# Index scores moved into a projection slot, the key norm's root and its sums moved in their queues

## The chip, the core and the metric

The kernel runs on one core of a Trainium2 chip. Its engines run side by side and meet only at semaphores: TensorE (PE) multiplies, ScalarE (ACT) and VectorE (DVE) work on elements, GpSimd (POOL) helps with elements, SyncE (SP) starts transfers. The metric is the device time of one execution, in microseconds (us); lower is better. All numbers are float32. Where a product has to be exact to float32, both operands are split into a rounded part (fp32r) and the rest, and three products are added.

## The reference

Two model blocks follow one another on 256 tokens of width 1024. The change lies in the last attention of the second block, the sparse one (DSA); what matters of it:

```python
proj = h @ w_in                       # 1024 x 2376: c_q 256, k 1024, v 1024, k_idx 64, w_idx 8
c_q = rms_norm(c_q, cq_g)
q = (c_q @ w_uq).reshape(B, S, 16, 64)
q_idx = apply_partial_rope((c_q @ w_uq_idx).reshape(B, S, 8, 64), cos, sin)
k_idx = apply_partial_rope(rms_norm(k_idx), cos, sin)
q = apply_partial_rope(rms_norm(q, q_g), cos, sin) * (d ** -0.5)
k = apply_partial_rope(rms_norm(k.reshape(B, S, 16, 64), k_g), cos, sin)
# for each block of 128 queries
dots  = einsum('bqhe,bke->bqhk', q_idx, k_idx)            # 8 index heads
score = einsum('bqh,bqhk->bqk', w_idx, relu(dots))        # + causal mask by chunks of 64
vals, idx = top_k(score, 64)
p = softmax(q . k[idx])                                   # 16 heads
o = p . v[idx];   return o @ w_out
```

Before it stand the differential attention and its MLP (`mlp0`), behind it the output projection `o3` and the last MLP (`mlp1`).

## The kernel before

The order of all work is written out by hand, one program for each engine; each runs its own list from top to bottom, and a wait holds up everything that stands behind it on that engine.

**Slots.** A weight matrix is read in slots of 1024 x 512 (1 MB) into `ringA`, which holds two. ScalarE rounds half a slot to fp32r (`round_slot`, writes `Ah`), VectorE or GpSimd makes the rest `Al = ringA - Ah` (`rest_slot`), and TensorE multiplies (`split_slot`, L786 to L834): for each half, 8 products `hTh, Ah` (both token tiles `t`, four parts `k`), 8 products `hTl, Ah`, 8 products `hTh, Al`. The last product of a tile counts up `job_rdy`; ScalarE then takes the 128 x 512 result out of PSUM (`sin_out`) and counts up `job_out`. `Ah` has two halves, so the rounding of a half waits until TensorE is done with the same half of the slot before (`a_free`).

**The DSA projection** has five slots, `sin` 0 to 4 (slot 4 has 328 columns). Behind slot 1 come the queries and index queries from the latent (L1474). Inside slot 2, between its halves, TensorE turns the index queries and keys (`index_aside`). The keys `s_k` are columns of slots 0, 1 and 2, the values `s_v` of 2, 3 and 4. GpSimd makes `Al` of slots 3 and 4.

**Index scores and top-k.** For each of 8 index heads TensorE multiplies two pieces into PSUM bank `i % 3` (L1485, L1486), ScalarE applies Relu (L2040), and VectorE adds it with its weight to `s_acc` (L2921, L2923). The three hand on in a ring: head `i` on TensorE waits for the Relu of head `i - 3` (`ixr`), the Relu for VectorE's addition of head `i - 2` (`ixs`). VectorE then finds the 64 largest of each row in 8 rounds of `max` and `match_replace` (L2937, L2940), and makes the mask `s_sel` (L2943, L2944).

**Key norm.** ScalarE squares the keys (L2044, counts up `osq`); VectorE sums the squares per head (`head_sums`, L2798) ahead of top-k round 3; ScalarE takes the root (`head_root("sk", 1)`, the call of `root` at L1523); VectorE scales and rotates the keys (`head_scale`, `rope2`, ahead of round 6; L2804, L2807, L2699 to L2704). TensorE turns the result (`turn_blocks`, L1261) and the attention over 16 heads begins (L1277). Ahead of that turn stands filler, `keep(7, ...)`: seven products nobody reads (L759).

**Queries.** TensorE turns them inside slot 3 (`query_aside`); ScalarE copies them out with `turned_queries` (eight instructions of L1686), then come `sin_out(3)` and the rounding of slot 4's second half, and behind these the key norm's root.

Of the kernel before, what the change touches and what calls it, by code (L numbers as in the profile page):

```python
# [28 lines left out]
P = 128  # L29
T = 256  # L30
# [15 lines left out]
IDX_H = 8  # L46
# [36 lines left out]
def program(nc, d, out_d):  # L83
# [4 lines left out]
    with ctx:  # L88
# [41 lines left out]
        def col(name, k):  # L130
            return cols[:, COL[name][0] + k:COL[name][0] + k + 1]
# [57 lines left out]
        job_rdy = sem("job_rdy")  # L189
# [122 lines left out]
        def in_job(w, c):  # L312
            at, name = (4, "din2") if w == "din" else (2, "sin2")
            return J[name][0] + 2 * (c - at) if c >= at else J[w][0] + 2 * c
# [408 lines left out]
        def _(pe):  # L723
# [32 lines left out]
            def keep(n, b):  # L756

                for _ in range(n):
                    mm(ps[:, b, 0:T], ident, con[:, 0:T], start=True, stop=True)  # L759
# [5 lines left out]
            def job_bank(j):  # L765
                if j >= 4:
                    pe.wait_ge(job_out, j - 3)
                return bank(j)
# [14 lines left out]
                        j += 1  # L783
                    off += n

            def split_slot(a, banks, name=None, done=None, between=None):  # L786

                n = A[a][0][2]  # L790
                for half in range(2):
                    ks = range(4 * half, 4 * half + 4)
                    pe.wait_ge(ah_rdy, 2 * SPLIT[a] + half + 1)

                    def product(t, left, right, start=False, stop=False, ready=None, ks=ks):
                        for k in ks:
                            if ready is not None and name and t == 0 and k % 2 == 0:
                                pe.wait_ge(ready, 4 * TI[name] + k // 2 + 1)
                            ins = mm(ps[:, banks[t], 0:n], left[:, k, t * P:(t + 1) * P],  # L799
                                     right[:, half, (k % 4) * n:(k % 4) * n + n],  # L800
                                     start=(start and k == 0), stop=(stop and k == KT - 1))
                        return ins

                    if done is m_rdy and half == 1:
                        pe.wait_ge(al_rdy, 2 * SPLIT[a] + half + 1)
                        for t in range(NT):
                            product(t, hTh, Ah)
                            product(t, hTl, Ah)
                            product(t, hTh, Al, stop=True).then_inc(m_rdy, 1)
                        continue  # L810
                    if name and half == 0:
                        for k in ks:
                            for t in range(NT):
                                product(t, hTh, Ah, start=True, ready=ha_rdy, ks=[k])
                        pe.wait_ge(al_rdy, 2 * SPLIT[a] + 1)
                        for t in range(NT):
                            product(t, hTh, Al)
                        for t in range(NT):
                            last = product(t, hTl, Ah, ready=hv_rdy)
                    else:  # L820
                        for t in range(NT):
                            product(t, hTh, Ah, start=True, ready=ha_rdy)
                        for t in range(NT):
                            product(t, hTl, Ah, ready=hv_rdy)
                        pe.wait_ge(al_rdy, 2 * SPLIT[a] + half + 1)
                        for t in range(NT):
                            last = product(t, hTh, Al, stop=True)
                            if half == 1 and done is not None:
                                last.then_inc(done, 1)
                    if half == 0 or done is None:  # L830
                        last.then_inc(a_used, 1)
                    if half == 0 and between is not None:
                        between()
# [7 lines left out]
                split_slot(a, (0, 2), name="o%d" % n)  # L841
                split_slot(a + 1, (1, 3), done=m_rdy)

            def split_jobs(a, j0, name=None, between=None):
                banks = (0, 1) if name else (job_bank(j0), job_bank(j0 + 1))
                split_slot(a, banks, name, job_rdy, between)

            def ffn(w, nf):

# [577 lines left out]
            def half(ap, u):  # L1427
                return ap[64 * (u % 2):64 * (u % 2) + 64, u // 2, :]
# [30 lines left out]
                pe.wait_ge(pre["hq"], 1)  # L1459
                turn_aside(0, [(lambda t, k=k: s_q[:, t, k * P:(k + 1) * P]) for k in range(8)])  # L1460

            def sin_jobs(s, between=None):
                split_jobs(a_at["sin"] + s, in_job("sin", s), "n3" if s == 0 else None, between)

            turn16("n3")
            sin_jobs(0)
# [3 lines left out]
            for j, off in ((J["uqx"][0], 1024), (J["uqq"][0], 0), (J["uqq"][0] + 2, 512)):  # L1470
                for t in range(NT):
# [2 lines left out]
                        last = mm(ps[:, b, :], s_cqT[:, k, t * P:(t + 1) * P],  # L1474
                                  s_uq[:, k, off:off + 512], start=(k == 0), stop=(k == 1))
                    last.then_inc(job_rdy, 1)
            sin_jobs(2, index_aside)
            pe.wait_ge(pre["sme"], 4)
            for i in range(IDX_H):
                if i >= 3:  # L1480
                    pe.wait_ge(pre["ixr"], i - 2)
                b = i % 3
                q = half(s_QIT, i)
                kx = s_KIT[64 * (i % 2):64 * (i % 2) + 64, :]
                mm(ps[:, b, 0:P], q[:, 0:P], kx[:, 0:P], start=True, stop=True)  # L1485
                mm(ps[:, b, P:3 * P], q[:, P:T], kx, start=True, stop=True).then_inc(pre["ix"], 1)  # L1486
            sin_jobs(3, query_aside)
            sin_jobs(4)
            keep(7, job_bank(J["k3"][0]))
            pe.wait_ge(pre["src"], 3)  # L1490
            turn_blocks(J["k3"][0], [((lambda t, k=k: s_k[:, t, k * P:(k + 1) * P]), P)
                                     for k in range(8)])
# [11 lines left out]
        def _(act):  # L1504
# [69 lines left out]
            def head_root(name, i):  # L1574

                root(name, st[:, 192 + 32 * i:224 + 32 * i], st[:, 128 + 32 * i:160 + 32 * i], HD, eps)
# [33 lines left out]
            def round_slot(a, half):  # L1610

                act.wait_ge(a_loaded[a % 2], 32 * (a // 2 + 1))
                n = 2 * SPLIT[a] + half
                if n >= 2:
                    act.wait_ge(*a_free[n - 2])
                nc.scalar.copy(k_half(Ah[:, half, :], a, 0), k_half(ringA[:, a % 2, :], a, half)  # L1616
                               ).then_inc(ah_rdy, 1)
# [56 lines left out]
            def aside(n, b, *copies):  # L1674

                act.wait_ge(pre["sm"], n)
                for f in copies:
                    last = f(ps[:, b, :])
                last.then_inc(pre["sme"], 1)

            def turned_queries(put, qz, gain, n):

                act.wait_ge(pre["gt"], 1)
                act.wait_ge(qz_rdy, n)
                for s in range(4):
                    put(s, *[lambda p, i=i: A_(  # L1686
                        pairs(qz)[64 * i:64 * i + 64, 2 * s:2 * s + 2, i, :],
                        p[64 * i:64 * i + 64, :].rearrange("p (k t) -> p k t", k=2),
                        ACT.Copy, scale=gain[64 * i:64 * i + 64, :])
                        for i in range(2)])  # L1690
# [314 lines left out]
            def sin_out(s):  # L2005
                w = min(512, DSA_IN - 512 * s)
                for t in range(NT):
                    job(in_job("sin", s) + t,
                        lambda p: scaled(s_p[:, t, s * 512:s * 512 + w], p[:, 0:w], t),
                        b=None if s else t)  # L2010
# [21 lines left out]
                    s_QIT[:, 2 * s:2 * s + 2, :].rearrange("p h t -> p (h t)"), p))  # L2032
            aside(4, 2, lambda p: nc.scalar.copy(s_KIT, p[:, 0:T]))
            round_slot(sin + 3, 0)
            sin_out(2)
            for i in range(IDX_H):
                act.wait_ge(pre["ix"], i + 1)
                if i >= 2:
                    act.wait_ge(pre["ixs"], i - 1)
                A_(s_ixr[:, i % 2, :], ps[:, i % 3, 0:384], ACT.Relu).then_inc(pre["ixr"], 1)  # L2040
            round_slot(sin + 3, 1)
            round_slot(sin + 4, 0)
            for t in range(NT):
                last = A_(s_sq[:, 2048 + t * 1024:3072 + t * 1024], s_k[:, t, :], ACT.Square)  # L2044
            last.then_inc(pre["osq"], 1)
            turned_queries(lambda s, *f: aside(5 + s, s, *f), s_QZ, col("sqk", 0), 2)
            sin_out(3)
            round_slot(sin + 4, 1)
            head_root("sk", 1)
            sin_out(4)  # L2050
            turned_keys(J["k3"][0])
            attend(2, s_soft)
# [86 lines left out]
        def _(dve):  # L2139
# [788 lines left out]

            m8 = st[:, 32:48]
            for r in range(TOPK // 8):  # L2930
                if r == 3:
                    head_sums(1, s_sq, 4)
                elif r == 6:
                    head_scale("sk", s_k)
                    rope2(s_k, H, s_rt, gains=3, done=pre["src"])
                for t, (lo, hi) in enumerate(((0, P), (P, 384))):
                    ins = V.max(m8[:, 8 * t:8 * t + 8], s_w[:, lo:hi])  # L2937
                link(ins)
                for t, (lo, hi) in enumerate(((0, P), (P, 384))):
                    ins = V.match_replace(s_w[:, lo:hi], m8[:, 8 * t:8 * t + 8], s_w[:, lo:hi], TAKEN)  # L2940
                link(ins)
# [108 lines left out]
```

## Time and profile before

| | us |
|---|---|
| median of 3 runs (1445.91 to 1447.65) | 1446.06 |
| the profiled execution | 1446.83 |
| span of its instructions | 1444.8 |
| TensorE busy | 1396.4 (97%) |
| VectorE busy | 933.9 (65%) |
| ScalarE busy | 629.1 (44%) |
| GpSimd busy | 52.1 (4%) |
| mean granted TensorE clock | 0.991 |

Times in the trace are us from the first instruction of the profiled execution; 2.03 us of that execution lie outside the span. In a timeline a row is one or more instructions of one kind: start, length, what it is, and in brackets the idle time of the engine before it with the instruction whose end ended that idle time. Ends of TensorE's products are modelled and overlap the next start, so a stretch of products is measured from start to start. A product of plain float32 operands shows as two instructions, one of fp32r operands as one. "Granted clock" is 1.00 at 2.4 GHz and 0.50 at 1.2 GHz.

### The profile page before, as it was taken

How to read it: one execution, taken by the hardware profiler on the slowest of the kernel's cores; microseconds unless marked ns; L12 is line 12 of the kernel's file. 1: busy time of each engine (PE TensorE's matmuls, PEld its weight loads, DVE VectorE, ACT ScalarE, POOL GpSimd, SP SyncE). 2: the span in 40 equal slices, each digit the busy share in tenths (PEclk: the TensorE clock that was granted, in tenths of full speed). 3: DMA queues.
4: the chain of work that ended last, by engine and by line, in shares of the span. 5: the costliest groups of instructions: out<-in, count | busy, mean ns of one | idle time of the engine just before them, and what ended most of it. 6: DMA issues, size and time to landing. Idle time of an engine off the chain costs nothing.

```text
span 1444.8 us, 22272 instructions
## 1 busy us (share of the span) xinstructions
PE 1396.4 (97%) x8796; PEld 1233.8 (85%) x8796; DVE 933.9 (65%) x1658; ACT 629.1 (44%) x944; POOL 52.1 (4%) x43
## 2 busy tenths in 40 slices
PE   7999999999999899999999999999999999999998
PEld 5886999789999798899999788789998688889997
DVE  5386467677767676577767678665554677565554
ACT  2232222364344556554333557554332668444331
POOL 1002000000000002000000000000000042000000
PEclk9999999999999898999999999999999999999999
DMA  6423101275553232365565252486441413365610
GB/s 229 172 89 117 59 2 59 73 237 187 174 191 132 103 102 92 127 200 188 176 199 173 66 199 89 140 314 231 177 172 59 154 59 117 147 252 185 218 73 29
DMA packets 110798, 208.14 MB, mean 144 GB/s; under 512 B 3808, under 2 KB 53088, under 8 KB 110208
## 3 DMA queue, kind: packets, MB, share of 16 engines
q1 hardware_dynamic: 110720, 207.06, 41.1%
q8 instruction: 54, 0.88, 0.2%
q14 instruction: 24, 0.20, 0.0%
HBM read 205.99 MB, written 1.05 MB: 143 GB/s over the span
## 4 chain that ended last, share of the span: by engine, by line
PE 88%; ACT 5%; DVE 5%; issue 1%; DMA 0%; SPq 0%; DVEq 0%; ACTq 0%
PE ps L903 20%; PE ps L799 12%; PE ps L884 9%; PE ps L889 9%; PE ps L881 9%; PE ps L1118 4%; PE ps L939 3%; PE ps L950 2%; PE ps L1235 2%; PE ps L1219 1%; PE ps L1278 1%; PE ps L862 1%; PE ps L1292 1%; PE ps L1389 1%; PE ps L1474 1%
## 5 line engine op out<-in xcount | busy, mean ns | idle before, releaser
L1626 ACT CAST Ah<-ringA 128x2048 fp32r<-128x2048 f32 x76 | 145.1, 1909 | 275.4 <-PE ps L889 258.4
L2254 DVE TENSOR_TENSOR Al<-ringA,Ah 128x2048 fp32r<-128x2048 f32 x76 | 174.2, 2292 | 98.6 <-ACT Ah L1626 98.4
L2261 DVE TENSOR_TENSOR Bl<-ringB,Bh 128x1024 fp32r<-128x1024 f32 (+1 forms) x76 | 127.0, 1671 | 52.6 <-ACT Bh L1635 52.5
L884 PE MATMUL ps<-hTl,Ah 128*128 128x256 f32 x1152 | 160.4, 281 | 0.0
L889 PE MATMUL ps<-hTh,Al 128*128 128x256 f32 x1152 | 159.9, 281 | 0.0
L881 PE MATMUL ps<-hTh,Ah 128*128 128x256 f32 x1152 | 159.7, 281 | 0.0
L1635 ACT CAST Bh<-ringB 128x1024 fp32r<-128x1024 f32 (+1 forms) x76 | 107.4, 1413 | 113.1 <-PE ps L903 112.8
L881 PEld LDWEIGHTS ps<-hTh,Ah 128*128 128x128 f32 x1152 | 151.0, 188 | 5.3
L884 PEld LDWEIGHTS ps<-hTl,Ah 128*128 128x128 f32 x1152 | 147.2, 189 | 0.0
L889 PEld LDWEIGHTS ps<-hTh,Al 128*128 128x128 f32 x1152 | 146.2, 189 | 0.0
L903 PE MATMUL ps<-Bh,hidh 128*128 128x512 f32 x432 | 135.1, 394 | 8.1 <-issue 6.6
L903 PE MATMUL ps<-Bl,hidh 128*128 128x512 f32 x432 | 134.1, 391 | 0.0
L903 PE MATMUL ps<-Bh,hidl 128*128 128x512 f32 x432 | 133.7, 391 | 0.0
L2247 DVE TENSOR_TENSOR Al<-ringA,Ah 128x2048 fp32r<-128x2048 f32 x30 | 68.6, 2289 | 44.6 <-ACT Ah L1616 44.5
L903 PEld LDWEIGHTS ps<-Bl,hidh 128*128 128x128 f32 x432 | 81.5, 189 | 17.9
L903 PEld LDWEIGHTS ps<-Bh,hidl 128*128 128x128 f32 x432 | 81.4, 188 | 17.6
L903 PEld LDWEIGHTS ps<-Bh,hidh 128*128 128x128 f32 x432 | 76.3, 189 | 21.1 <-issue 9.6
L1616 ACT CAST Ah<-ringA 128x2048 fp32r<-128x2048 f32 (+1 forms) x38 | 71.2, 1875 | 43.2 <-PE ps L799 39.7
L2280 DVE TENSOR_SCALAR xn<-ps,cols 128x256 f32<-128x256 f32 x44 | 23.9, 544 | 79.2 <-PE ps L889 79.2
L799 PE MATMUL ps<-Ah,hTh 128*128 128x512 f32 (+1 forms) x288 | 73.6, 395 | 1.3 <-ACT Ah L1616 0.4
L799 PE MATMUL ps<-Al,hTh 128*128 128x512 f32 (+1 forms) x288 | 72.4, 391 | 0.5 <-POOL Al L2100 0.5
L799 PE MATMUL ps<-Ah,hTl 128*128 128x512 f32 (+1 forms) x288 | 70.9, 386 | 0.0
(410 smaller groups left out, 2178.0 us busy)
## 6 DMA issues: line engine op xcount, KB each, us to landing
ringA<-in_ffn_w_in SPq DMA_DIRECT2D x44, 1024.0 KB, 7.5
ringA<-in_mlp_w SPq DMA_DIRECT2D x32, 1024.0 KB, 7.5
ringB<-in_mlp_w SPq DMA_DIRECT2D x32, 1024.0 KB, 6.9
ringB<-in_ffn_w_out SPq DMA_DIRECT2D x44, 512.0 KB, 4.1
ringA<-in_diff_w_in SPq DMA_DIRECT2D x12, 1024.0 KB, 6.7
ringA<-in_dsa_w_in SPq DMA_DIRECT2D x8, 1024.0 KB, 6.2
ringA<-in_w_k SPq DMA_DIRECT2D x4, 1024.0 KB, 8.5
ringA<-in_w_r SPq DMA_DIRECT2D x4, 1024.0 KB, 6.3
```

The source lines that it names most:

```text
L799: ins = mm(ps[:, banks[t], 0:n], left[:, k, t * P:(t + 1) * P], right[:, half, (k % 4) * n:(k % 4) * n + n], start=(start and k == 0), sto ...
L881: mm(o, Ah[:, half, k * T + j * P:k * T + j * P + P], hTh[:, k, :], start=(k == 0), stop=False)
L884: mm(o, Ah[:, half, k * T + j * P:k * T + j * P + P], hTl[:, k, :], start=False, stop=False)
L889: last = mm(o, Al[:, half, k * T + j * P:k * T + j * P + P], hTh[:, k, :], start=False, stop=(k == KT - 1))
L903: last = mm(ps[:, 2 * t + c_, :], hb[:, half, f * T + t * P:f * T + t * P + P], wb[:, half, o:o + 512], start=(first_one and f == 0 and i ...
L1118: last = mm(ps[:, b, q * w:(q + 1) * w], L[lhs][:, q * P:(q + 1) * P], L[rhs][:, q * w:(q + 1) * w], start=True, stop=True)
L1616: nc.scalar.copy(k_half(Ah[:, half, :], a, 0), k_half(ringA[:, a % 2, :], a, half)).then_inc(ah_rdy, 1)
L1626: nc.scalar.copy(a_split(w, Ah, half), a_half(w, ap, half)).then_inc(ah_rdy, 1)
L1635: nc.scalar.copy(Bh[:, half, 0:n], ringB[:, bp, half * n:(half + 1) * n]).then_inc(bh_rdy, 1)
L2247: V.tensor_tensor(k_half(Al[:, half, :], a, 0), k_half(ringA[:, a % 2, :], a, half), k_half(Ah[:, half, :], a, 0).bitcast(F32), ALU.subtra ...
L2254: V.tensor_tensor(a_split(w, Al, half), a_half(w, (a_at[w] + par) % 2, half), a_split(w, Ah, half).bitcast(F32), ALU.subtract).then_inc(al ...
L2261: V.tensor_tensor(Bl[:, half, 0:n], ringB[:, (G0[w] + par) % 2, half * n:(half + 1) * n], Bh[:, half, 0:n].bitcast(F32), ALU.subtract).the ...
```

## The change

It has four parts, all in the DSA stage. (1) On TensorE the index scores no longer stand behind slot 2: `split_slot` has a new argument `inside`, called in the second half behind its first 8 products, and `index_scores` is passed there for slot 2. (2) On ScalarE `sin_out(2)` moves behind the eight Relus, and the key norm's root moves from behind slot 4's second rounding to directly behind the squares, ahead of `turned_queries`. A wait of ScalarE on its own `job_out` is written ahead of the squares. (3) On VectorE `head_sums` for the keys stands ahead of round 4 instead of round 3. (4) The filler ahead of the key turn is 2 products instead of 7.

```diff
-            def split_slot(a, banks, name=None, done=None, between=None):
+            def split_slot(a, banks, name=None, done=None, between=None, inside=None):
...
                         for t in range(NT):
                             product(t, hTh, Ah, start=True, ready=ha_rdy)
+                        if half and inside is not None:
+                            inside()
                         for t in range(NT):
                             product(t, hTl, Ah, ready=hv_rdy)
...
+            def index_scores():
+                pe.wait_ge(pre["sme"], 4)
+                for i in range(IDX_H):
+                    if i >= 3:
+                        pe.wait_ge(pre["ixr"], i - 2)
...
-            sin_jobs(2, index_aside)
-            pe.wait_ge(pre["sme"], 4)
-            for i in range(IDX_H):
...
+            sin_jobs(2, index_aside, index_scores)
             sin_jobs(3, query_aside)
             sin_jobs(4)
-            keep(7, job_bank(J["k3"][0]))
+            keep(2, job_bank(J["k3"][0]))
...
             round_slot(sin + 3, 0)
-            sin_out(2)
             for i in range(IDX_H):
...
                 A_(s_ixr[:, i % 2, :], ps[:, i % 3, 0:384], ACT.Relu).then_inc(pre["ixr"], 1)
+            sin_out(2)
             round_slot(sin + 3, 1)
             round_slot(sin + 4, 0)
+            act.wait_ge(job_out, in_job("sin", 2) + 2)
             for t in range(NT):
                 last = A_(s_sq[:, 2048 + t * 1024:3072 + t * 1024], s_k[:, t, :], ACT.Square)
             last.then_inc(pre["osq"], 1)
+            head_root("sk", 1)
             turned_queries(lambda s, *f: aside(5 + s, s, *f), s_QZ, col("sqk", 0), 2)
             sin_out(3)
             round_slot(sin + 4, 1)
-            head_root("sk", 1)
             sin_out(4)
...
             for r in range(TOPK // 8):
-                if r == 3:
+                if r == 4:
                     head_sums(1, s_sq, 4)
```

TensorE before, from the second half of slot 2 to slot 3 (six more pairs of index products stand at the dots):

```order
L799 MATMUL ps<-Ah,hTh 128x512 x8
L799 MATMUL ps<-Ah,hTl 128x512 x8
L799 MATMUL ps<-Al,hTh 128x512 x8
L1485 MATMUL ps<-arena,ringB 128x128
L1486 MATMUL ps<-arena,ringB 128x256
...
L1486 MATMUL ps<-arena,ringB 128x256
L799 MATMUL ps<-Ah,hTh 128x512 x8
```

TensorE after, the same stretch; line numbers have moved, L1472 and L1473 are the index products:

```order
L799 MATMUL ps<-Ah,hTh 128x512 x8
L1472 MATMUL ps<-arena,ringB 128x128
L1473 MATMUL ps<-arena,ringB 128x256
...
L1473 MATMUL ps<-arena,ringB 128x256
L799 MATMUL ps<-Ah,hTl 128x512 x8
L799 MATMUL ps<-Al,hTh 128x512 x8
L799 MATMUL ps<-Ah,hTh 128x512 x8
```

The sixteen index products now stand ahead of sixteen of slot 2's own products, and nothing else moved.

ScalarE before, from the taking out of slot 2 to the key norm's root (L1616 rounds, L1559 takes a slot out, L2040 is the Relu, L2044 the squares, L1686 the query copies, L1523 the root):

```order
L1559 ACTIVATE arena<-ps,st 128x512 x2
L2040 ACTIVATE arena<-ps 128x384 x8
L1616 CAST Ah<-ringA 128x2048
L1616 CAST Ah<-ringA 128x1312
L2044 ACTIVATE rows<-arena 128x1024 x2
L1686 ACTIVATE ringB<-ps,cols 64x2x256 x8
L1559 ACTIVATE arena<-ps,st 128x512 x2
L1616 CAST Ah<-ringA 128x1312
L1523 ACTIVATE st<-st,con 128x32
```

ScalarE after, from the Relus to the taking out of slot 3, where the same are L1622, L1565, L2045, L2051, L1692 and L1529:

```order
L2045 ACTIVATE arena<-ps 128x384 x8
L1565 ACTIVATE arena<-ps,st 128x512 x2
L1622 CAST Ah<-ringA 128x2048
L1622 CAST Ah<-ringA 128x1312
L2051 ACTIVATE rows<-arena 128x1024 x2
L1529 ACTIVATE st<-st,con 128x32
L1692 ACTIVATE ringB<-ps,cols 64x2x256 x8
L1565 ACTIVATE arena<-ps,st 128x512 x2
```

The taking out of slot 2 went behind the Relus, and the root went ahead of the eight query copies, the taking out of slot 3 and the rounding of slot 4's second half.

## Rows read from the trace of the kernel before

**Rows 1.** the page, section 4: the chain that ended last, by engine

```profile
PE 88%; ACT 5%; DVE 5%; issue 1%; DMA 0%; SPq 0%; DVEq 0%; ACTq 0%
```

**Rows 2.** timeline of TensorE, slot 2; start us, us, engine, line, operation, tiles, count, [idle before]

```profile
1163.14 1.98 PE L799 MATMUL ps<-Ah,hTl 128*128 128x512 f32 x8
...
1166.92 0.50 PE L1485 MATMUL ps<-arena,ringB 64*128 64x128 f32 x4
...
1172.12 2.14 PE L799 MATMUL ps<-Ah,hTh 128*128 128x512 f32 x8
```

**Rows 3.** timeline of ScalarE, from slot 2 to the root of the key norm

```profile
1162.04 1.93 ACT L1616 CAST Ah<-ringA 128x2048 fp32r<-128x2048 f32 x1
1166.10 0.69 ACT L1559 ACTIVATE arena<-ps,st 128x512 f32<-128x512 f32 x1 [2.13 <-PE ps L799]
...
1167.87 0.87 ACT L2040 ACTIVATE arena<-ps 128x384 f32<-128x384 f32 x2 [0.16 <-PE ps L1486]
...
1178.06 1.29 ACT L1616 CAST Ah<-ringA 128x1312 fp32r<-128x1312 f32 x1 [2.70 <-PE ps L799]
1179.25 2.01 ACT L2044 ACTIVATE rows<-arena 128x1024 f32<-128x1024 f32 x2
1181.17 5.58 ACT L1686 ACTIVATE ringB<-ps,cols 64x512 f32<-64x512 f32 x8
...
1187.93 1.28 ACT L1616 CAST Ah<-ringA 128x1312 fp32r<-128x1312 f32 x1
1189.11 0.33 ACT L1523 ACTIVATE st<-st,con 128x32 f32<-128x32 f32 x1
```

**Rows 4.** timeline of VectorE, from the index scores to the mask

```profile
1168.47 0.60 DVE L2921 TENSOR_SCALAR arena<-arena 128x128 f32<-128x128 f32 x2 [5.03 <-ACT arena L2040]
...
1175.18 0.62 DVE L2937 MAX8 st<-arena 128x8 f32<-128x128 f32 x2
...
1176.61 0.62 DVE L2937 MAX8 st<-arena 128x8 f32<-128x128 f32 x2
...
1181.36 2.29 DVE L2798 TENSOR_REDUCE st<-rows 128x32 f32<-128x2048 f32 x1 [1.91 <-ACT rows L2044]
...
1189.53 0.35 DVE L2804 RECIPROCAL st<-st 128x32 f32<-128x32 f32 x1 [1.70 <-ACT st L1523]
...
1197.20 0.28 DVE L2704 TENSOR_TENSOR arena<-arena 128x128 f32<-128x128 f32 x1
...
1200.66 0.36 DVE L2944 TENSOR_SCALAR arena<-arena 128x384 f32<-128x384 f32 x1
```

**Rows 5.** timeline of TensorE, slot 4, filler and key turn

```profile
1187.51 1.36 PE L799 MATMUL ps<-Al,hTh 128*128 128x328 f32 x8
...
1189.27 1.47 PE L799 MATMUL ps<-Ah,hTh 128*128 128x328 f32 x8 [0.39 <-ACT Ah L1616]
...
1192.40 1.47 PE L799 MATMUL ps<-Al,hTh 128*128 128x328 f32 x8 [0.46 <-POOL Al L2100]
1193.71 3.18 PE L759 MATMUL ps<-con 128*128 128x256 f32 x14
1197.54 1.97 PE L1261 MATMUL ps<-con,arena 128*128 128x128 f32 x16 [0.65 <-DVE arena L2704]
```

**Rows 6.** windows of TensorE: stretch, length, busy, granted clock, DMA share, GB/s

```profile
1271.50:1274.50 3.00, 3.00 (x7) 0.50 0.25 90
...
497.00:506.00 9.00, 5.99 (x22) 0.50 0.01 2
1160.00:1202.00 42.00, 39.62 (x221) 1.00 0.28 101
```

**Rows 7.** timeline of TensorE behind that gap, second part of mlp1

```profile
1271.46 1.19 PE L903 MATMUL ps<-Bh,hidh 128*128 128x512 f32 x2 [2.79 <-issue]
...
1274.93 0.63 PE L903 MATMUL ps<-Bl,hidh 128*128 128x512 f32 x2
...
1276.78 0.62 PE L903 MATMUL ps<-Bh,hidl 128*128 128x512 f32 x2
```

More of the change, by code:

```diff
@@ L842, in out_proj, with split_jobs @@
                 split_slot(a + 1, (1, 3), done=m_rdy)
-            def split_jobs(a, j0, name=None, between=None):
+            def split_jobs(a, j0, name=None, between=None, inside=None):
                 banks = (0, 1) if name else (job_bank(j0), job_bank(j0 + 1))
-                split_slot(a, banks, name, job_rdy, between)
+                split_slot(a, banks, name, job_rdy, between, inside)
             def ffn(w, nf):
@@ L1460, in query_aside, with sin_jobs @@
                 turn_aside(0, [(lambda t, k=k: s_q[:, t, k * P:(k + 1) * P]) for k in range(8)])
-            def sin_jobs(s, between=None):
-                split_jobs(a_at["sin"] + s, in_job("sin", s), "n3" if s == 0 else None, between)
+            def index_scores():
[3 more added lines that the diff above has]
+                        pe.wait_ge(pre["ixr"], i - 2)
+                    b = i % 3
+                    q = half(s_QIT, i)
+                    kx = s_KIT[64 * (i % 2):64 * (i % 2) + 64, :]
+                    mm(ps[:, b, 0:P], q[:, 0:P], kx[:, 0:P], start=True, stop=True)
+                    mm(ps[:, b, P:3 * P], q[:, P:T], kx, start=True, stop=True
+                       ).then_inc(pre["ix"], 1)
+            def sin_jobs(s, between=None, inside=None):
+                split_jobs(a_at["sin"] + s, in_job("sin", s), "n3" if s == 0 else None, between,
+                           inside)
             turn16("n3")
@@ L1476, in _ @@
                     last.then_inc(job_rdy, 1)
-            sin_jobs(2, index_aside)
-            pe.wait_ge(pre["sme"], 4)
-            for i in range(IDX_H):
[L1480 to L1486, printed above, removed]
+            sin_jobs(2, index_aside, index_scores)
             sin_jobs(3, query_aside)
             sin_jobs(4)
-            keep(7, job_bank(J["k3"][0]))
+            keep(2, job_bank(J["k3"][0]))
             pe.wait_ge(pre["src"], 3)
```

## The prediction

> **What bounds the kernel now.** I read the page first, then the DSA stage in the timelines engine by engine, then windows with the granted clock. The chain that ended last is 88% TensorE [rows 1], so an edit is worth what it takes from TensorE's own list or from its waits. The change adds and removes no product but filler. What it can shorten is the wait in which the chain leaves TensorE: ahead of the key turn. There the profile shows this. TensorE ends slot 4 at 1193.71, does 3.18 us of filler, waits 0.65 us more and turns the keys from 1197.54 [rows 5]. It waits for VectorE's scaling and rotation, which ends at 1197.48 and began at 1189.53 after 1.70 us of waiting for ScalarE's root [rows 4]; and that root started at 1189.11 only because it stands behind 5.58 us of query copies, slot 3's results and a rounding [rows 3]. So the end of the stage is set by squares, sums, root, scaling. The filler is cover and no work: with the keys earlier, up to 1197.54 - 1193.71 = 3.83 us are there to be taken.
>
> **Part 1, index scores inside slot 2.** TensorE's index products started at 1166.92, behind the 16 products that follow 1163.14; now they start at about 1163.14, 3.78 us earlier [rows 2]. What feeds them is there: ScalarE's last rounding ends at 1163.97 and the first Relu ran 0.95 us behind the first product, so now at 1164.09 [rows 2, 3]. The three engines pass the heads round in a ring; all of it moves by 3.78 us and keeps its 5.20 us on TensorE (1166.92 to 1172.12), since VectorE's pace in it does not change. The 16 products come behind, and slot 3 starts at 1172.12 as before: TensorE's own sum is 0. I allow -0.1 to +0.3 us for a ring that starts with ScalarE just out of its rounding.
>
> VectorE gets the 3.78 us. Its first addition comes at 1164.69, its first top-k round at 1171.40 instead of 1175.18 [rows 4].
>
> **Part 2, slot 2's results behind the Relus.** They are complete 5.20 us later, so ScalarE takes them from 1171.3 instead of 1166.10 [rows 3]; the Relus are over by then. Slot 3's second rounding follows at once, near 1172.8, and ends before TensorE has finished slot 3's first half, which is what ended ScalarE's wait of 2.70 us at 1178.06. That wait swallows the rest: the rounding of slot 4's first half is tied to TensorE, which is not earlier, and the squares behind it start again at 1179.25 and end at 1181.26 [rows 3]. Worth 0. This is the point on which I think the gain is lost: the squares are not VectorE's to hasten.
>
> **Part 3, sums one round later.** A round takes 1176.61 - 1175.18 = 1.43 us. Four rounds from 1171.40 end at 1177.1. The sums still start at 1181.36, 0.10 us behind the squares, and last 2.29 us [rows 4]. VectorE waits 4.2 us there instead of 1.91. Two rounds follow, to 1186.5, then scaling and rotation with their 7.95 us (1189.53 to 1197.48): keys ready at 1194.4, 3.1 us earlier. The root is no longer waited for: it can be had at 1183.98. The two last rounds (2.9) and the mask (two instructions like the one that ended at 1201.02, 0.36 us each) end near 1198.1, 2.9 us before they did.
>
> **Part 4, the root ahead of the query copies.** The root takes 0.33 us, but the wait in it costs more. ScalarE ends the squares at 1181.26, VectorE's sums end at 1183.65, so ScalarE stands 2.4 us with everything queued behind: query copies, slot 3's results, the rounding of slot 4's second half. The copies started at 1181.17 and now start at 1183.93, 2.76 us later. All of that queue moves by 2.76: the rounding from 1187.93 to 1190.69, ending near 1192.0 [rows 3]. TensorE was waiting for it already, 0.39 us, and started at 1189.27; now it starts at 1192.03. GpSimd's rest, which ended a second wait of 0.46 us at 1192.40, comes at 1195.16, and slot 4 ends at 1196.47 instead of 1193.71 [rows 5].
>
> **Part 5, filler.** Seven filler products are 14 instructions in 3.18 us, 0.23 each; two are 0.91 us [rows 5]. The key turn starts at 1196.47 + 0.91 = 1197.38, the keys having been there since 1194.4. Against 1197.54 that is -0.16 us. The chain behind (key copies, scores, softmax) keeps its lengths.
>
> **The clock.** Between slot 4's halves TensorE now stands from 1188.87 to 1192.03, 3.2 us instead of 0.4. The trace has one gap of that kind in dense work: 2.79 us ahead of 1271.46, after which the granted clock was 0.50 from 1271.5 to 1274.5 [rows 6, 7], that is 1.2 GHz instead of 2.4. The four pairs from 1271.46 to 1274.93 took 3.47 us, the next four, to 1276.78, 1.85: it cost 1.62 us [rows 7]. Here 0.46 us of that would hide in the wait for GpSimd's rest, which leaves at most 1.16; where the clock falls earlier in the gap less work is hit, down to 0. I take 1.0, near the row's end, since its gap was shorter than this one. [...]
>
> **The sum.** 0 - 0.16 + 1.0 = +0.8 us on the profiled execution's 1446.83, so 1447.6. That execution is 0.77 us above the median of 1446.06; against the median I forecast 1446.9.
>
> **Rivals.**
>
> A. The clock holds: all as above without the 1.0, -0.16 us, 1445.9. For it: the index ring, the filler and the turns all ran at 1.00 in this stage [rows 6]. Against: the gap is eight times as long as the one of before, and longer than the one that did cost the clock.
>
> B. The gain comes through. If the rounding of slot 4 is not late, TensorE ends slot 4 at 1193.71, the filler at 1194.62, and the keys are ready at 1194.4: -2.9 us, 1443.1. For it: VectorE's side really is 3.1 us earlier. Against: it needs squares some 2 us earlier than 1179.25, and what stands ahead of them waited 2.70 us for TensorE [rows 3].
>
> C. Slower: the clock falls in the gap and does not come back with slot 4's last products, as in the trace's other long stretch, where it was 0.50 over all of 497 to 506 though TensorE was busy for 6.0 of the 9 us [rows 6]. From 1192.03 on there are 4.0 us of products (1189.27 to 1193.71 less 0.46), 0.9 of filler and 2.0 of turns; 9 us at half speed lose 4.5, less 0.46 hidden and 0.16 gained: +3.9, 1450.0. It decides from the point where the low clock lasts beyond slot 4, about 1196.5. Against: slot 4's products are dense, like those behind 1271.46, and these had it back within 3.5 us.
>
> **How the numbers follow.** Forecast 0.45, A 0.33, B 0.07, C 0.09, and 0.06 for things between. A run of this kernel can be told from no change from about 0.2%, 2.9 us. Forecast and A are both far inside, B lies just at the edge, C beyond it: faster 0.08, same 0.83, slower 0.09. The range leaves out B and C: from A less 1.0 (half the spread of 1.74 us of the three runs, and 0.1 of part 1) to A plus two low stretches of the clock at their full 1.62 each: 1444.9 to 1449.1.
>
> **What would show it.** In the profile after: first Relu near 1164.1, first top-k round near 1171.4, squares still near 1179.2, VectorE idle some 4.2 us ahead of the sums, ScalarE idle 2.4 us ahead of a root near 1183.7, query copies from 1183.9, TensorE idle about 3.2 us between slot 4's halves, ended by ScalarE's rounding, key turn near 1197.4 with no wait of its own (or up to 1.2 later with a granted clock of 0.50 just ahead). I am wrong if the squares come earlier, if TensorE's gap in slot 4 stays under 1 us, or if the key turn starts before 1196.

## The result, and the profile after

The kernel after the change takes 1453.52 us (median of 5 runs, 1451.19 to 1454.79), the kernel before 1447.65 (median of 5, 1445.91 to 1447.80) beside it. The ratio is 1.0042 [1.0030, 1.0055]: slower by 0.4%, above the predicted range.

| kernel | profiled execution | span | granted clock, mean |
|---|---|---|---|
| before | 1446.83 | 1444.8 | 0.991 |
| after | 1454.79 | 1452.6 | 0.988 |

The spans differ by 7.8 us. To place it I take three marks of TensorE: the first products of slot 2's second half, the first of slot 3, and the key turn.

| stretch | before | after | difference |
|---|---|---|---|
| start to slot 2's second half | 1161.20 | 1163.52 | +2.32 |
| to slot 3 | 10.92 | 16.70 | +5.78 |
| to the key turn | 25.42 | 25.12 | -0.30 |
| to the end | 247.26 | 247.26 | 0.00 |

The 2.32 us ahead of the stage are not the change's. 0.74 us of them are there when TensorE comes out of a wait near 952 us, in code that is the same in both kernels. The other 1.58 us come just behind that wait, where the profiled execution of after had a stretch of low clock that the one of before had not. TensorE's row behind the wait, and a window over it, before:

```profile
951.99 0.70 PE L903 MATMUL ps<-Bh,hidh 128*128 128x512 f32 x2 [2.79 <-issue]
950.00:958.00 8.00, 6.01 (x28) 1.00 1.04 399
```

and after (the columns of the windows are those of [rows 6]):

```profile
952.73 1.19 PE L905 MATMUL ps<-Bh,hidh 128*128 128x512 f32 x2 [2.79 <-issue]
950.00:958.00 8.00, 5.27 (x16) 0.79 1.04 396
```

The wait is 2.79 us long in both; the clock stayed at 1.00 in one and fell in the other. Of the eleven profiled executions of this document nine have the low stretch in this window (0.73 to 0.82), and those of before and `mid_only` have not. The 21 runs of before beside the first experiments spread from 1445.51 to 1448.77. So a median can stand some 2 us off from what one stage gained or lost, and below I judge every kernel by the two distances within the stage, and by the ratio.

The chain of the page after answers to [rows 1] and tells as little of the cause:

```profile
PE 87%; ACT 5%; DVE 5%; issue 1%; DMA 0%; POOL 0%; SPq 0%; DVEq 0%; ACTq 0%; POOLq 0%
```

TensorE after, in its timeline; these are the rows that answer to [rows 2, 5]:

```profile
1163.52 2.12 PE L799 MATMUL ps<-Ah,hTh 128*128 128x512 f32 x8
1165.57 0.50 PE L1472 MATMUL ps<-arena,ringB 64*128 64x128 f32 x4
...
1171.95 0.79 PE L1472 MATMUL ps<-arena,ringB 64*128 64x128 f32 x2 [3.58 <-ACT arena L2045]
...
1175.09 3.43 PE L799 MATMUL ps<-Ah,hTl 128*128 128x512 f32 x8
1178.36 2.03 PE L799 MATMUL ps<-Al,hTh 128*128 128x512 f32 x8
1180.22 2.03 PE L799 MATMUL ps<-Ah,hTh 128*128 128x512 f32 x8
...
1200.01 1.48 PE L799 MATMUL ps<-Ah,hTh 128*128 128x328 f32 x8 [3.13 <-ACT Ah L1622]
...
1205.34 1.91 PE L1263 MATMUL ps<-con,arena 128*128 128x128 f32 x16
```

The new wait is 3.58 us long and lies inside the index products, ahead of 1171.95. It is ended by a Relu of ScalarE; and behind it eight products of slot 2 take 1178.36 - 1175.09 = 3.27 us, where the same eight took 1.8 before. The windows over these rows show why:

```profile
1160.00:1171.00 11.00, 8.37 (x50) 1.00 0.00 0
1171.50:1177.50 6.00, 5.55 (x18) 0.50 0.01 1
1178.00:1200.00 22.00, 18.87 (x99) 1.00 0.27 96
```

The granted clock is 1.00 up to the gap, 0.50 behind it (1.2 GHz instead of 2.4), and 1.00 again from 1178, ahead of slot 2's last eight products. Against the three parts of before (1.94 us for the first 8 products, 5.20 for the ring, 3.78 for the 16 products) the stretch now has 2.05, 9.52 and 5.13: +0.11, +4.32, +1.35.

The Relu that TensorE waited for was itself kept waiting. ScalarE after (answers to [rows 3]):

```profile
1171.40 0.49 ACT L2045 ACTIVATE arena<-ps 128x384 f32<-128x384 f32 x1 [4.01 <-DVE arena L2928]
...
1186.06 1.29 ACT L1622 CAST Ah<-ringA 128x1312 fp32r<-128x1312 f32 x1 [3.15 <-PE ps L799]
...
1191.68 0.32 ACT L1529 ACTIVATE st<-st,con 128x32 f32<-128x32 f32 x1 [2.42 <-DVE st L2805]
```

Its third Relu stood idle for 4.01 us, until VectorE's first instruction in the ring was done. VectorE after (answers to [rows 4]):

```profile
1167.12 4.20 DVE L2928 TENSOR_SCALAR arena<-arena 128x128 f32<-128x128 f32 x2 [1.36 <-ACT arena L2045]
1171.35 5.45 DVE L2930 SCALAR_TENSOR_TENSOR arena<-arena 128x128 f32<-128x128 f32 x14
...
1177.42 0.62 DVE L2944 MAX8 st<-arena 128x8 f32<-128x128 f32 x2
...
1189.36 2.29 DVE L2805 TENSOR_REDUCE st<-rows 128x32 f32<-128x2048 f32 x1 [6.22 <-ACT rows L2051]
...
1194.82 2.36 DVE L2814 TENSOR_TENSOR arena<-arena,st 128x1024 f32<-128x1024 f32 x2
```

This is the row to look at. The two scalings of head 0 (128 and 256 columns) took 0.60 us before [rows 4] and 4.20 now. VectorE has no idle time in the page's sense there: the instruction is booked as busy. What ran at that time is in GpSimd's timeline, which the prediction never read for this place:

```profile
1166.46 4.50 POOL L2107 TENSOR_TENSOR Al<-ringA,Ah 128x2048 fp32r<-128x2048 f32 x1 [39.59 <-ACT Ah L1622]
```

GpSimd subtracts the rounded part of slot 3's first half (line 2107) from 1166.46 to 1170.96. VectorE's first instruction began at 1167.12, 0.66 us behind it, and came to its end when GpSimd did. In the kernel before the same rest stood here:

```profile
1164.14 4.58 POOL L2100 TENSOR_TENSOR Al<-ringA,Ah 128x2048 fp32r<-128x2048 f32 x1 [39.60 <-ACT Ah L1616]
...
1189.36 2.99 POOL L2100 TENSOR_TENSOR Al<-ringA,Ah 128x1312 fp32r<-128x1312 f32 x1 [6.13 <-ACT Ah L1616]
```

It ended at 1168.72, and the first scaling began at 1168.47: the two overlapped by 0.25 us only. Moving the ring 3.78 us ahead put that scaling at 1164.69, 0.55 us behind the start of those 4.58 us. So the engines do not meet only at semaphores, as the opening has it: no semaphore stands between these two instructions.

A second such row was in the trace of before, and the prediction took it as it stood:

```profile
1189.92 4.64 DVE L2807 TENSOR_TENSOR arena<-arena,st 128x1024 f32<-128x1024 f32 x2
```

The two multiplications with the key norm's root take 4.64 us beside GpSimd's rest from 1189.36 to 1192.35, and 2.36 in the kernel after, where nothing of GpSimd lies beside them. "7.95 us for scaling and rotation" contained 2.3 us of being held.

### The profile page after: what moved, and what is told of

It reads as the page before. It is cut to its first block, busy times and chain, and to the rows that moved or that the text cites. A ratio compares the mean times of both kernels' runs of the same rounds, so it can differ in the third digit from the quotient of the medians.

```text
span 1452.6 us, 22252 instructions
## 1 busy us (share of the span) xinstructions
PE 1397.3 (96%) x8786; PEld 1235.1 (85%) x8786; DVE 935.1 (64%) x1658; ACT 629.2 (43%) x944; POOL 52.0 (4%) x43
## 4 chain that ended last, share of the span: by engine, by line
PE 87%; ACT 5%; DVE 5%; issue 1%; DMA 0%; POOL 0%; SPq 0%; DVEq 0%; ACTq 0%; POOLq 0%
PE ps L905 20%; PE ps L799 12%; PE ps L886 9%; PE ps L891 9%; PE ps L883 9%; PE ps L1120 4%; PE ps L941 3%; PE ps L952 2%; PE ps L1237 2%; PE ps L1221 1%; PE ps L864 1%; PE ps L1280 1%; PE ps L1391 1%; PE ps L1294 1%; PE ps L1489 1%
## 5 line engine op out<-in xcount | busy, mean ns | idle before, releaser
L1622 ACT CAST Ah<-ringA 128x2048 fp32r<-128x2048 f32 (+1 forms) x38 | 71.2, 1874 | 43.6 <-PE ps L799 40.2
```

## The experiments

Theory P: VectorE and GpSimd keep each other out of SBUF, one instruction at a time, and the low clock follows from the gap that this makes on TensorE. Rival I: the place inside slot 2 is bad in itself (ScalarE only just out of its rounding, psum buffers of the ring, the products split up). Rival R: ScalarE's stall for the root costs the time, as case C had it. All kernels, in the order of the text (the distances are those of the table above, in the profiled execution; each ratio is to runs of before taken beside that kernel, whose median was 1447.65 for after, 1447.68 for `root_mid` and `squares_early`, 1447.85 for `mid_only` and `combined`, and 1447.76 for the others):

| kernel | median us (range, runs) | ratio to before | slot 2's second half to slot 3 | to the key turn |
|---|---|---|---|---|
| before | 1447.76 (1445.51 to 1448.77, 21) | | 10.92 | 25.42 |
| after | 1453.52 (5) | 1.0042 [1.0030, 1.0055] | 16.70 | 25.12 |
| index_only | 1453.44 (1450.68 to 1454.58, 5) | 1.0046 [1.0032, 1.0060] | 17.36 | 25.32 |
| queues_only | 1448.23 (1446.79 to 1450.81, 11) | 1.0012 [1.0003, 1.0021] | 10.94 | 26.00 |
| rest_in_ring | 1454.31 (1452.35 to 1454.85, 5) | 1.0053 [1.0039, 1.0066] | 15.84 | 26.32 |
| rest_behind | 1445.70 (1444.65 to 1449.99, 11) | 0.9997 [0.9988, 1.0006] | 11.00 | 26.06 |
| root_mid | 1443.95 (1441.88 to 1445.06, 9) | 0.9975 [0.9965, 0.9985] | 11.00 | 22.93 |
| mid_only | 1443.70 (1441.74 to 1444.51, 7) | 0.9970 [0.9959, 0.9981] | 10.92 | 22.89 |
| squares_early | 1444.07 (1442.48 to 1445.47, 11) | 0.9976 [0.9967, 0.9985] | 10.93 | 20.93 |
| combined | 1441.62 (1440.96 to 1443.74, 5) | 0.9961 [0.9947, 0.9975] | 11.01 | 20.54 |

**The change in two halves.** `index_only` is parts 1 and 2 of the prediction (the kernel after with the root, the sums and the filler put back):

```diff
-            keep(2, job_bank(J["k3"][0]))
+            keep(7, job_bank(J["k3"][0]))
...
-            head_root("sk", 1)
             turned_queries(...)
             sin_out(3)
             round_slot(sin + 4, 1)
+            head_root("sk", 1)
...
-                if r == 4:
+                if r == 3:
                     head_sums(1, s_sq, 4)
```

> The first half of the change alone: index scores inside slot 2 and slot 2's results behind the Relus; root, sums and filler as before. Port theory (GpSimd's rest of slot 3 holds VectorE's first addition): the addition lasts near 4 us again, TensorE waits near 3.6 us inside the ring, time +4 to +6 us over before (+0.3 to +0.4%). Rival 1 (the loss is ScalarE's stall for the early root): no long addition matters, time within 1 us of before. Rival 2 (clock alone): the addition may be long but time is +1 to +2.

It has the whole loss: 1.0046. The held instruction is there again, and the eight products behind it take 3.6 us. VectorE of `index_only`:

```profile
1163.82 4.20 DVE L2928 TENSOR_SCALAR arena<-arena 128x128 f32<-128x128 f32 x2 [1.35 <-ACT arena L2045]
```

`queues_only` is the same edit made to the kernel before in the other direction: parts 3 to 5 alone.

> The second half alone: root ahead of the query copies, sums ahead of round 4, two fillers; index scores as before. Port theory: no addition is held; ScalarE waits 2.4 us ahead of the root, TensorE near 3 us between slot 4's halves, key turn -0.2 to +1.0 us, time within 1 us of before. Rival 1 (ScalarE's stall): +4 to +6 us.

Slot 3 starts where it did (10.94), the key turn 0.58 us later; the ratio is just above 1. TensorE in slot 4, in its timeline, and its window behind the gap (in the gap itself, from 1188 to 1191, the granted clock was 1.00):

```profile
1191.50 2.00 PE L799 MATMUL ps<-Ah,hTh 128*128 128x328 f32 x8 [3.14 <-ACT Ah L1616]
1193.30 2.39 PE L799 MATMUL ps<-Ah,hTl 128*128 128x328 f32 x8
1195.49 1.43 PE L799 MATMUL ps<-Al,hTh 128*128 128x328 f32 x8
```

```profile
1192.00:1195.00 3.00, 3.00 (x14) 0.53 0.00 0
```

Here the clock fell behind a gap of 3.14 us, as the forecast had it, and the first 16 products took 3.99 us (2.6 at the full clock). So rival R is true for 0.6 us of the stage and no more (the whole execution has a ratio of 1.0012 [1.0003, 1.0021]): the loss is in the index part.

**The rest put into the ring, with nothing else moved.** `rest_in_ring` is the kernel before, in which GpSimd's first rest of slot 3 waits for VectorE's first addition:

```diff
             for s in (3, 4):
                 for half in range(2):
+                    if (s, half) == (3, 0):
+                        pool.wait_ge(pre["ixs"], 1)
                     rest_slot(a_at["sin"] + s, half)
```

> The kernel before with one change on GpSimd alone: its rest of slot 3's first half waits until VectorE's first addition is done, so it runs inside the ring of index scores. Port theory in full (any VectorE operation that reads two tensors from SBUF is held): the additions behind the first are held, one of them lasts near 4.5 us, ring and slot 3 +4 us, time +4 to +6 us. Port theory for TENSOR_SCALAR only, or rival (the place inside the slot is the cause): additions stay at 0.39 us each, time as before.

TensorE's and ScalarE's lists are those of before, the index scores stand behind slot 2, and the root is late: what rivals I and R need is absent. It is as slow as the change, 1.0053. GpSimd, VectorE and TensorE:

```profile
1168.81 4.61 POOL L2100 TENSOR_TENSOR Al<-ringA,Ah 128x2048 fp32r<-128x2048 f32 x1 [44.60 <-DVE arena L2923]
```

```profile
1168.12 0.55 DVE L2923 TENSOR_SCALAR arena<-arena 128x128 f32<-128x128 f32 x2 [5.03 <-ACT arena L2040]
1168.71 9.69 DVE L2925 SCALAR_TENSOR_TENSOR arena<-arena 128x128 f32<-128x128 f32 x14
```

```profile
1174.34 0.79 PE L1485 MATMUL ps<-arena,ringB 64*128 64x128 f32 x2 [4.11 <-ACT arena L2040]
...
1176.69 3.03 PE L799 MATMUL ps<-Ah,hTh 128*128 128x512 f32 x8
```

The two scalings take their 0.55 us, since GpSimd is not yet at work; the 14 additions, of which one meets it, take 9.69 us instead of 5.45. TensorE has its gap (4.11 us) and the slow products behind it, now slot 3's.

**The rest taken out of the ring, with the change kept.** `rest_behind` is the kernel after with `pool.wait_ge(pre["ixs"], 8)` at the same place: GpSimd begins when the ring is over.

> The changed kernel with GpSimd's rest of slot 3's first half held until the eighth addition is done. Port theory: first addition 0.3 us, no wait of TensorE inside the ring, slot 3 at its old distance, time -0.2 to +1.0 us against before, 5 us below the changed kernel. Rivals (place inside the slot, or ScalarE's stall): as slow as the changed kernel.

The loss of slot 2 is gone: 11.00 to slot 3, where before has 10.92, and a ratio of 0.9997 [0.9988, 1.0006]. VectorE, GpSimd and TensorE:

```profile
1164.14 0.55 DVE L2930 TENSOR_SCALAR arena<-arena 128x128 f32<-128x128 f32 x2 [1.35 <-ACT arena L2045]
1164.73 5.45 DVE L2932 SCALAR_TENSOR_TENSOR arena<-arena 128x128 f32<-128x128 f32 x14
```

```profile
1170.31 12.76 POOL L2107 TENSOR_TENSOR Al<-ringA,Ah 128x2048 fp32r<-128x2048 f32 x3 [46.41 <-DVE arena L2932]
```

```profile
1191.50 2.27 PE L799 MATMUL ps<-Ah,hTh 128*128 128x328 f32 x8 [3.13 <-ACT Ah L1622]
1193.57 2.14 PE L799 MATMUL ps<-Ah,hTl 128*128 128x328 f32 x8
```

With 0.55 and 5.45 us in the ring the place inside slot 2 costs 0.08 us, within the allowance of the prediction. Rival I falls. In slot 4 the root's stall of ScalarE makes the gap of 3.13 us, and the first eight products take 2.07 instead of 1.3.

**Which operations are held.** `op_probe` has an appendix behind the kernel's end: GpSimd adds two 128x1024 tiles over and over (2.34 us each), and each time VectorE does two top-8 searches and then one operation on 64 columns beside it (the kernel before runs ahead of it, so that its 1470.98 us mean nothing). It is one execution, with one instruction of each kind.

```diff
+            kinds = [lambda o: V.tensor_copy(o, src[:, 0:64]),
+                     lambda o: V.tensor_scalar(o, src[:, 0:64], 2.0, None, ALU.mult),
+                     lambda o: V.tensor_tensor(o, src[:, 0:64], two[:, 0:64], ALU.add),
...
+            for k in range(10):
+                if k >= 1:
+                    pool.wait_ge(pre["pd"], k - 1)
+                G.tensor_tensor(ringA[:, 0, 0:1024], ringA[:, 1, 0:1024], ringA[:, 1, 1024:2048],
+                                ALU.add).then_inc(pre["pg"], 1)
```

> The kernel before with a probe behind its end: GpSimd adds two SBUF tensors (128 x 1024, 2.3 us) nine times, and beside each VectorE does two max and then one operation of one kind on 64 columns. Port theory: held until GpSimd's operation ends (2 us instead of 0.2) are tensor_copy and tensor_scalar from SBUF and tensor_tensor, scalar_tensor_tensor of two SBUF tensors; not held are those with one tensor in PSUM, tensor_reduce, max; reciprocal open. Rival (GpSimd slows all of VectorE): all are long.

VectorE, and one of GpSimd's rows:

```profile
1446.76 1.70 DVE L2969 COPY xn<-xn 128x64 f32<-128x64 f32 x1
...
1449.11 1.88 DVE L2970 TENSOR_SCALAR xn<-xn 128x64 f32<-128x64 f32 x1
...
1451.65 2.25 DVE L2971 TENSOR_TENSOR xn<-xn 128x64 f32<-128x64 f32 x1
...
1454.53 1.94 DVE L2972 SCALAR_TENSOR_TENSOR xn<-xn,st 128x64 f32<-128x64 f32 x1
...
1457.09 0.20 DVE L2973 TENSOR_TENSOR xn<-xn,ps 128x64 f32<-128x64 f32 x1
...
1464.49 0.20 DVE L2976 TENSOR_REDUCE xn<-xn 128x1 f32<-128x64 f32 x1
```

```profile
1448.61 2.34 POOL L2140 TENSOR_TENSOR ringA<-ringA 128x1024 f32<-128x1024 f32 x1 [0.20 <-DVE xn L2969]
```

The first four (a copy, a scaling, an addition of two tiles and a fused one, all with operands in SBUF) last 1.70 to 2.25 us, and each ends with the GpSimd instruction beside it: the scaling at 1450.99, GpSimd at 1450.95. The others do not wait: an addition with one operand in PSUM 0.20, a scaling out of PSUM 0.21, reciprocal 0.53, a sum along the row 0.20, the top-8 0.21. That fits the top-k rounds and the key sums, which ran beside GpSimd at their usual length in the traces here. The Trainium skill (SBUF — State Buffer, section "Who interferes with whom") says so: an instruction of VectorE with two inputs in SBUF, or one in a mode that uses both ports (copies and scalings can be), needs a pair of ports that it shares with GpSimd when GpSimd reads SBUF, and whichever is issued first has it for its whole length. The runs agree, with these numbers.

**Where the expected 3 us are.** The prediction found VectorE's side 3.1 us earlier and the gain lost in ScalarE's stall. `root_mid` is `rest_behind` with the root between the fourth and fifth block of query copies (`head_root` called inside the loop at s == 2), so that ScalarE need not wait for the sums.

> rest_behind with the root between the fourth and the fifth query copy instead of ahead of all eight. Port theory with ScalarE's stall as second cost: the sums are done when ScalarE gets to the root, so the wait of 3.1 us between slot 4's halves goes (0.4 to 0.8 left) and the clock stays up; GpSimd's last rest then runs from 1189.7 to 1192.7 beside the key norm's rotation, whose two-tensor operations are held by it, so keys near 1195.2 instead of 1197.5 and the time -2 to -2.5 us against before. If nothing of SBUF is shared: keys at 1194.4, -2.7 us. Rival (the stall hides nothing, the end is set elsewhere): as rest_behind, within 1 us of before.

TensorE waits 0.75 us in slot 4 instead of 3.13, and the key turn comes 2.4 us earlier than before: rival B's size. VectorE's rotation meets the last rest of GpSimd (1191.84, 3.08 us) and is held, 3.10 us for an instruction of 0.28. That costs nothing here: the keys are ready at 1197.05, and TensorE comes to the key turn out of its own list, with no wait, at 1197.15. It would be the next limit, 0.10 us away, if the two filler products went:

```profile
1191.96 3.10 DVE L2715 TENSOR_TENSOR arena<-arena,gt 128x128 f32<-128x128 f32 x1
```

`mid_only` asks whether the early ring has any part in this: the kernel before with the root in mid-copies, sums at round 4 and two filler products.

> The kernel before with three moves: root between the fourth and fifth query copy, sums ahead of round 4, two fillers; index scores as before. Theory: VectorE's 3.8 us from the early ring were idle in root_mid, so this gains the same -2.3 to -2.5 us. Rival (the early ring carries the gain): -1 us or less.

25.42 becomes 22.89, against 22.93 with the ring early; the ratios, 0.9970 and 0.9975, overlap. The early index scores carry nothing here.

`squares_early` starts from the kernel before too and cuts at the squares: they stand ahead of slot 3's second rounding, the sums at round 1, the root behind slot 4's first rounding, the scaling at round 4, slot 4's last rest on VectorE instead of GpSimd, and no filler.

```diff
-            round_slot(sin + 3, 1)
-            round_slot(sin + 4, 0)
+            act.wait_ge(job_out, in_job("sin", 2) + 2)
             for t in range(NT):
                 last = A_(s_sq[:, 2048 + t * 1024:3072 + t * 1024], s_k[:, t, :], ACT.Square)
             last.then_inc(pre["osq"], 1)
+            round_slot(sin + 3, 1)
+            round_slot(sin + 4, 0)
+            head_root("sk", 1)
...
                     rope2(s_k, H, s_rt, gains=3, done=pre["src"])
+                    dve.wait_ge(al_rdy, 2 * SPLIT[a_at["sin"] + 4] + 1)
+                    rest_slot(a_at["sin"] + 4, 1)
```

> A version made from the kernel before: squares ahead of slot 3's second rounding, where ScalarE waited 2.7 us; root behind slot 4's first rounding; sums ahead of round 1, scaling and rotation ahead of round 4, when GpSimd has ended its rests; the last rest of slot 4 on VectorE; no filler. Theory: TensorE's 0.39, 0.46 and 0.65 us of waits and 3.18 us of filler go, key turn near 1193 instead of 1197.5, mask near 1196.8, time -3.5 to -4.5 us (-0.25 to -0.3%). If the mask becomes late: -3. Rival (the keys did not set the end): within 1 us of before.

The key turn is 4.48 us earlier, but 1.21 of it are given back: from the key turn to the first product behind a softmax it is 6.93 us, and 5.72 before. The ratio, 0.9976, cannot be told from the 0.9975 of `root_mid`. TensorE waits 1.94 us for the softmax, which waits for the mask, whose last instruction VectorE starts at 1197.31. TensorE and VectorE:

```profile
1192.61 1.91 PE L1261 MATMUL ps<-con,arena 128*128 128x128 f32 x16
...
1199.54 0.55 PE L1292 MATMUL ps<-con,arena 128*128 128x128 f32 x3 [1.94 <-ACT arena L1864]
```

```profile
1197.31 0.36 DVE L2945 TENSOR_SCALAR arena<-arena 128x384 f32<-128x384 f32 x1
```

Here the early ring should have a use, since it brings the mask forward. `combined` is the kernel after with GpSimd's first rest behind the ring, squares, root, last rest and filler as in `squares_early`, sums at round 3 and scaling at round 6.

> The changed kernel (index scores inside slot 2) with GpSimd's first rest behind the ring, squares ahead of slot 3's second rounding, root behind slot 4's first rounding, sums ahead of round 3, scaling and rotation ahead of round 6, slot 4's last rest on VectorE, no filler. Theory: in squares_early the mask was 2 us late; here VectorE is 3.8 us earlier, so mask near 1193.5 and the end is TensorE's alone: key turn 4.9 us earlier than before, time -4.5 to -5 us (-0.33%). Rival (starting the ring early is worth nothing): as squares_early, -3.3 to -3.6 us.

TensorE, VectorE and GpSimd:

```profile
1192.01 1.91 PE L1263 MATMUL ps<-con,arena 128*128 128x128 f32 x16
...
1197.68 0.55 PE L1294 MATMUL ps<-con,arena 128*128 128x128 f32 x3 [0.67 <-ACT arena L1870]
```

```profile
1193.83 0.36 DVE L2952 TENSOR_SCALAR arena<-arena 128x384 f32<-128x384 f32 x1
1195.84 0.35 DVE L2659 CUSTOM_DVE_ANT_0 arena<-ps,arena,st 128x128 f32<-128x128 f32 x1 [1.65 <-PE ps L1280]
```

```profile
1170.22 4.97 POOL L2106 TENSOR_TENSOR Al<-ringA,Ah 128x2048 fp32r<-128x2048 f32 x1 [46.41 <-DVE arena L2929]
```

The mask's last instruction starts at 1193.83, 3.5 us earlier than in `squares_early` (3.2 counted from slot 2's second half), and VectorE now waits for TensorE (1.65 us); the key turn is 4.79 us earlier than before and nothing of it is given back behind it (5.67 us from the key turn to 1197.68). At 1441.62 us, 0.9961 [0.9947, 0.9975], it is faster than before and after by more than the noise. Its interval overlaps that of `squares_early`, 0.9976 [0.9967, 0.9985], and it moves more than the ring, so what the early ring is worth here is read from the mask and the 1.26 us behind the key turn, and not shown by the times.

## Why the prediction was wrong

**The step that failed** stands in part 1: the ring "keeps its 5.20 us on TensorE, since VectorE's pace in it does not change". It took 9.52. The step asked whether the operands of the ring were there, and never what else ran on its new place. GpSimd's rest of slot 3 begins as soon as ScalarE's rounding ends, in both kernels, and VectorE's scalings and additions do not run beside it: they stand until it ends. Price: 4.32 us in the ring (about 3.6 of them the held instruction, the rest the low clock) and 1.35 us on slot 2's last 16 products, of which the first eight ran at the low clock. `rest_in_ring` makes the loss without the change, `rest_behind` keeps the change without the loss.

**Part 1's other terms** held: with GpSimd out of the way slot 3 starts 0.08 us later than before, predicted -0.1 to +0.3.

**Parts 2 and 3** were right in their order, late by the ring: the squares wait for TensorE (3.15 us ahead of 1186.06), and VectorE's wait ahead of the sums, put at 4.2 us, was 6.22: the squares had slipped by 5.7 us with TensorE, the top-k rounds by 3.7. In `root_mid`, where the ring is not held, it was 4.3.

**Part 4** held to a tenth: ScalarE waits 2.42 us for the root (2.4 predicted), TensorE 3.13 between slot 4's halves (3.2), GpSimd's rest ends a second wait of 0.48.

**Part 5**: the key turn had no wait of its own, as predicted. From slot 3 to the key turn the kernel after has -0.30 us, where the sum without the clock gave -0.16; the keys were ready at 1200.1, 5.2 us ahead of their turn, where the sum had 3.0. The rest is the hold that the 7.95 us of part 3 contained: the two multiplications took 2.36 us instead of 4.64.

**The clock** was right as a mechanism and uncertain as an event. It fell behind the gap of 3.13 us in `queues_only` and `rest_behind` (+0.58 and +0.64 us to the key turn, where 0.84 was forecast) and stayed at 1.00 through a gap of 3.13 us in the profiled execution of after. What decides it was not tried. The prediction had it that its trace holds one gap of this kind. It holds two: ahead of 951.99 TensorE stands 2.79 us as well, and there the clock stayed at 1.00. So the trace gave no lean towards the 1.0 us, and the 0.45 against 0.33 rested on one of two gaps.

**The rivals.** B's end state exists, 2.4 to 2.5 us in `root_mid` and `mid_only`; what kept the change from it, apart from the ring, was the stall of part 4, as the prediction said. But the prediction asked for squares 2 us earlier, and they were not needed: in `root_mid` the sums start 0.1 us later against slot 2 than before, and moving the root alone takes the stall away. C asked for a clock that stays low beyond slot 4, and no run has that. The mechanism that did decide was on no list: the probability given to "slower" came from the clock alone.

**What stays open.** The stage of `combined` is 4.79 us shorter, its median 6.2 us; the stage of `rest_behind` 0.72 longer, its median 2.1 us shorter, with an interval that holds 1. These differences lie outside the stage and are within the spread of before (3.3 us). What brings the stretch of low clock near 952 us in most executions and not in all is not settled.

## What to carry to other kernels

When work of VectorE is moved in time, lay GpSimd's timeline beside the new place and ask whether the VectorE instruction reads two operands from SBUF, or is a copy or a scaling within SBUF. GpSimd's instructions here all read two operands from SBUF; beside one of them such an instruction of VectorE waits for what is left of GpSimd's, and GpSimd's are the longer ones (the rest of 128x1312 took it 2.99 us, and VectorE 1.51 in `squares_early`). A long duration of a short instruction on VectorE (4.20 us for two of 0.3) can be a wait, though no view calls it one: compare the same form elsewhere in the trace before taking its length as work. And where three engines pass data round in a ring, such a hold on one of them can count twice: here 3.6 us as time and 2.1 us as TensorE's low clock behind the gap.

## What the runs showed of the hardware that I had not expected

VectorE is held until GpSimd's instruction ends, whatever the size of its own: 64 columns took up to 2.25 us, 128 columns 3.93. The sum along the row, the reciprocal, the top-8, and the one addition and the one scaling with an operand in PSUM were not held. The reverse seems to hold too: in `combined` GpSimd's rest began at 1170.22 beside VectorE's addition of the mask (1170.12 to 1170.68) and took 4.97 us, where it took 4.50 in the kernel after: 0.47 more, for 0.46 us of overlap. TensorE's clock fell to 0.50 at gaps of 3.58 and 4.11 us in the three traces that have them, and at gaps of 3.13 us in two traces of three. At the gap of 2.79 us near 952 it fell in nine profiled executions of eleven.
